# Five blocks per retention head, rotations counted by chunk, HGRN heads of 10 and 11 slots, ten Strassen pairs in the input projection

## The reference

```python
def _layer(...):
    h = _rms_norm(x, g_pre_mix)
    z = h @ w_in
    q_a, k_a, v_a, g_a, q_b, f_b, i_b, g_b, m_a, m_b = _split_cols(z)
    qa = _rope(q_a, pos); ka = _rope(k_a, pos) * (RET_DK ** -0.5)
    o_a, s_ret_new = _retention(qa, ka, va, s_ret, ret_chunk)
    y_a = (silu(g_a) * _head_rms(o_a)) @ w_a
    f = lbh + (1.0 - lbh) * sigmoid(f_b)
    o_b, s_hg_new = _hgrn2(qb, 1.0 - f, vb, jnp.log(f), s_hg, hg_block)
    y_b = (silu(g_b) * _head_rms(o_b)) @ w_b
    mix = sigmoid(m_a) * y_a + sigmoid(m_b) * y_b
    x = x + _rms_norm(mix @ w_out, g_post_mix)
    u = square(relu(_rms_norm(x, g_pre_ffn) @ w_up))
    return x + _rms_norm(u @ w_down, g_post_ffn), s_ret_new, s_hg_new
```

## Time and profile before

| | |
|---|---|
| median of 3 runs | 2351.37 us (2348.11 to 2351.53) |
| the profiled execution | 2349.41 us, its span 2347.6 us |
| mean granted TensorE clock | 0.998 |
| TensorE busy | 2325.4 us, 99% of the span |
| VectorE busy | 1378.4 us, 59% |
| ScalarE busy | 818.0 us, 35% |
| GpSimd busy | 477.9 us, 20% |

### The profile page before, as it was taken

One profiled execution on the slowest core, in us unless ns is written; L12 is line 12 of the kernel. 1 busy time (PEld: TensorE's weight loads), 2 busy tenths in 40 slices (PEclk: granted clock), 3 DMA queues, 4 the chain that ended last, 5 costly groups with the idle time before them and its releaser, 6 DMA issues. The chain is left out here.

```text
span 2347.6 us, 37061 instructions
## 1 busy us (share of the span) xinstructions
PE 2325.4 (99%) x14240; PEld 2184.5 (93%) x14240; DVE 1378.4 (59%) x2562; ACT 818.0 (35%) x1552; POOL 477.9 (20%) x732
## 2 busy tenths in 40 slices
PE   8999999999999999999999999999999999999998
PEld 7899999999999999999999999988999999888886
DVE  7434355362636777777776434556755556777575
ACT  5223232323222333333232332333555554333233
POOL 1000022221206666566655000000000000000002
PEclk9999999999999999999999999999999999999999
DMA  5212455353724343344334634222434436533424
GB/s 196 85 57 103 145 181 173 123 200 115 234 93 158 116 130 113 114 128 133 108 115 143 203 106 140 100 100 82 150 112 152 137 123 250 191 117 125 170 72 143
DMA packets 256044, 319.23 MB, mean 136 GB/s; under 512 B 10005, under 2 KB 200217, under 8 KB 255769
## 3 DMA queue, kind: packets, MB, share of 16 engines
q1 hardware_dynamic: 255464, 315.67, 40.1%
q0 software_dynamic: 432, 1.57, 0.4%
HBM read 205.53 MB, written 111.67 MB: 135 GB/s over the span
## 5 line engine op out<-in xcount | busy, mean ns | idle before, releaser
L942 PE MATMUL bank<-XH,WHI 128*128 128x384 f32 x1776 | 609.9, 343 | 1.6 <-issue 0.9
L944 PE MATMUL bank<-XH,WLO 128*128 128x384 f32 x1776 | 594.7, 335 | 0.0
L943 PE MATMUL bank<-XL,WHI 128*128 128x384 f32 x1776 | 593.9, 334 | 0.0
L942 PEld LDWEIGHTS bank<-XH,WHI 128*128 128x128 f32 x1776 | 333.8, 188 | 5.6 <-issue 2.4
L943 PEld LDWEIGHTS bank<-XL,WHI 128*128 128x128 f32 x1776 | 333.9, 188 | 0.8
L944 PEld LDWEIGHTS bank<-XH,WLO 128*128 128x128 f32 x1776 | 333.3, 188 | 0.0
L1396 ACT ACTIVATE ZST<-bank 128x384 f32<-128x384 f32 x180 | 88.3, 492 | 377.6 <-PE bank L944 371.8
L1330 PE MATMUL bank<-WSH,USH 128*128 128x512 f32 x448 | 175.3, 391 | 1.0 <-issue 1.0
L1332 PE MATMUL bank<-WSH,USL 128*128 128x512 f32 x448 | 175.3, 391 | 0.0
L1331 PE MATMUL bank<-WSL,USH 128*128 128x512 f32 x448 | 175.1, 391 | 0.0
L1396 ACT ACTIVATE WHI<-WRAW 128x1024 fp32r<-128x1024 f32 (+1 forms) x161 | 135.2, 842 | 114.0 <-PE bank L1057 70.3
(11 more groups left out here) (282 smaller groups left out, 5007.1 us busy)
## 6 DMA issues: line engine op xcount, KB each, us to landing
WRAW<-in_w_in SPq DMA_DIRECT2D x80, 512.0 KB, 4.6
scratch_z<-ZST SPq DMA_DIRECT2D x60, 576.0 KB, 3.2
UOP<-scratch_uq SPq DMA_DIRECT2D x28, 1024.0 KB, 7.4
WRAW<-in_w_up SPq DMA_DIRECT2D x32, 512.0 KB, 5.5
scratch_uq<-U SPq DMA_DIRECT2D x16, 1024.0 KB, 4.0
WQ<-in_w_down SPq DMA_DIRECT2D x16, 1024.0 KB, 5.2
scratch_uq<-SU SPq DMA_DIRECT2D x16, 768.0 KB, 5.5
HZ<-scratch_z SPq DMA_DIRECT2D x63, 192.0 KB, 2.9
```

What stands on the lines that cost most here:

```text
L942: pe.matmul(psum[c][:, 0:CH], WHI[p][:, k, :], XH[:, k, s], start=(k == 0), stop=False)
L943: pe.matmul(psum[c][:, 0:CH], WHI[p][:, k, :], XL[:, k, s], start=False, stop=False)
L944: last = pe.matmul(psum[c][:, 0:CH], WLO[p][:, k, :], XH[:, k, s], start=False, stop=(k == KT - 1))
```

## The change

NZ goes from 6 to 10: eight blocks that were plain become four Strassen pairs. Retention heads have five blocks (15 slots, RET_A = 4), and the two blocks of the gap stay as HG_START = 6 slots. HGRN heads have 10 and 11 slots in turn with pieces in slots 0 to 8; with 10 slots the last `out_t` of a head stands in slot 0 of the next. All loops over heads are unrolled. The rotation of q's chunk 0 moves to the end of the head before, chunks of q and k alternate over slots 0 to 4, and q_ok and k_ok count chunks. S8A gets memory of its own, KZ8 takes that of RTMP; ZK and ZV are loaded earlier. GpSimd's chunk 0 of the rotation of k moves to the end of the head before.

```diff
-RET_BLOCKS = 6
-RET_SLOTS = RET_BLOCKS * NC
-HG_BLOCKS = 4
-HG_SLOTS = HG_BLOCKS * NC
-RA = 7
-HG_A = (0, 1, 2, 4, 5, 6, 7, 8, 9)
-R_GATE = (7, 8, 13)
-H_GATE = (0, 2, 6)
+RET_LEN = (5, 5, 5, 5)
+RET_AT = (0, 5, 10, 15)
+RET_BLOCKS = sum(RET_LEN)
+HG_BLOCKS = 30
+HG_START = 6
+HG_LEN = (10, 11, 10, 11, 10, 11, 10, 11)
+HG_AT = [None] * HG_START + [(h, s) for h, n in enumerate(HG_LEN) for s in range(n)]
+RET_A = tuple(NC * n - 11 for n in RET_LEN)
+R_GATE = (1, 2, 6)
+H_GATE = (1, 2, 6)
...
-GAP = 2
-NZ = 7 - GAP // 2
+NZ = (72 - 2 - RET_BLOCKS - HG_BLOCKS) // 2
...
-        S8A = ZK[:, :, :].rearrange("p a t -> p (a t)")[:, 0:4 * 2 * RD].rearrange("p (b d e) -> p b d e", b=4, d=2)
-        KZ8 = [sb(f"KZ8{i}", [P, RD], F32, pr) for i in range(2)]
+        S8A = sb("S8A", [P, 4, 2, RD], F32, pr)
+        KZ8 = [RTMP[:, :, :].rearrange("p a n -> p (a n)")[:, b * RD:(b + 1) * RD] for b in range(2)]
...
+        def hg_slots():
+
+            for q, at in enumerate(HG_AT):
+                yield NHB + q // NC, q % NC, *(at or (None, None))
+
+        def hg_out(h, s):
+
+            if h is None:
+                return None
+            if s == 0:
+                return (h - 1, NT - 1) if h and HG_LEN[h - 1] == NT + 1 else None
+            return (h, s - 2) if 2 <= s < NT + 2 else None
...
+                    if j == late + 3 and h < RH - 1:
+                        sp.wait_ge(R.k_ok, 3 * h + 3)
+                        sp.wait_ge(R.q_ok, 3 * h + 3)
+                        z_stored(6 * h + 9 - 2 * NZ)
+                        load_rk(h + 1)
...
+                if t % TPC == 0:
+                    pe.wait_ge(R.q_ok, 3 * h + t // TPC + 1)
+                    pe.wait_ge(R.k_ok, 3 * h + t // TPC + 1)
                 if t == 0:
-                    pe.wait_ge(R.in_[2], 16 * h + 16)
-                    pe.wait_ge(R.q_ok, h + 1)
-                    pe.wait_ge(R.k_ok, h + 1)
                     pe.wait_ge(R.kz8, 2 * h + 1)
                     pe.wait_ge(R.st_ev, 16 * h + 1)
                 pe.wait_ge(R.kv, 8 * h + t + 1)
...
-            with dve.Fori(0, RH) as h:
-                for s in range(RET_SLOTS):
+            for h in range(RH):
+                RA = RET_A[h]
+                for s in range(NC * RET_LEN[h]):
                     j, c = divmod(s, NC)
-                    n = 2 + RET_BLOCKS * h + j
+                    n = 2 + RET_AT[h] + j
                     if c == 0:
-                        wlo_block(n + 1, (j + 1) % 2)
-                    if s < 3:
+                        wlo_block(n + 1, (n + 1) % 2)
+                    if s == 0 and h == 0:
+                        dve.wait_ge(R.in_[0], 32)
+                        rotate_q(0, 0)
+                    if s in (0, 2, 4):
                         if s == 0:
-                            dve.wait_ge(R.in_[0], 32 * h + 32)
-                        rotate_q(h, s)
-                    if s == 3:
-                        dve.wait_ge(R.in_[1], 16 * h + 16)
-                        for c in range(NC):
-                            rotate_k0(c)
+                            dve.wait_ge(R.in_[1], 16 * h + 16)
+                        rotate_k0(s // 2)
                         dve.sem_inc(R.q_ok, 1)
+                    if s in (1, 3):
+                        rotate_q(h, s // 2 + 1)
                     for t in range(NT):
                         if s == RA + t:
                             if t == 0:
@@ -2161,6 +2181,9 @@
                             dve.wait_ge(R.sc, 9 * h + t + 1)
                             dve.wait_ge(R.st_full, 16 * h + (t if t >= 2 else 1))
                             dve.tensor_tensor(ATT[t % 2][:, :], PSC[:, 0:P], DM[:, t // NTP, :], ALU.mult).then_inc(R.att, 1)
+                    if s == NC * RET_LEN[h] - 1 and h < RH - 1:
+                        dve.wait_ge(R.in_[0], 32 * h + 64)
+                        rotate_q(h + 1, 0)
...
+            for n, c, h, s in hg_slots():
+                end = HG_LEN[-1] - s if h == HH - 1 else None
+                if c == 0 and s != NT:
+                    wlo_block(n + 1, (n + 1) % 2)
+                if n == NHB and c == 0:
                     dve.wait_ge(c_in2, 48)
                     forget(0, 0)
                     prep_q(0, 0, 0)
                     prep_q(0, 0, 1)
                     dve.wait_ge(R.s8_st[0], 32 * RH + 16)
                     prep_q(0, 0, 2)
-                if n == NHB - GAP + 1:
+                if n == NHB + 1 and c == 0:
                     ret_done(dve)
                     forget(0, 1)
                     prep_q(1, 1, 0)
-            wlo_block(NHB + 1, 1)
+                if h is None:
+                    continue
+                if s == 0:
+                    ch.reset()
+                if s < NT:
+                    weights(h, s)
+                if end == 1:
+                    for x in range(6, 11):
+                        piece(x)
+                if hg_out(h, s):
+                    gated(H, *hg_out(h, s), 1)
+                if 1 <= s < NT:
+                    hg_state(h, s - 1)
+                if 1 <= s < NT + 1:
+                    head_ms(H, h, s - 1, HD)
+                if s == NT:
+                    hg_state(h, NT - 1)
+                    if c == 0:
+                        wlo_block(n + 1, (n + 1) % 2)
+                if s < 2:
+                    prep_q(1, (h + 1) % 2, s + 1)
+                if s == 2:
+                    forget(h, 2)
+                if 3 <= s <= 5:
+                    prep_q(2, h % 2, s - 3)
+                if h < HH - 1:
+                    if s == 6:
+                        forget(h + 1, 0)
+                    if 6 <= s <= 8:
+                        prep_q(0, (h + 1) % 2, s - 6)
+                    if s == 9:
+                        forget(h + 1, 1)
+                        prep_q(1, h % 2, 0)
...
+            def rotate_k1(c):
+
+                s = slice(c * CH, (c + 1) * CH)
+                cs, sn = CS[:, 0, s], CS[:, 1, s]
+                pool.tensor_tensor(PTMP[:, 0, :], ZK[:, 0, s], sn, ALU.mult)
+                ch(pool.tensor_tensor(PTMP[:, 1, :], ZK[:, 1, s], cs, ALU.mult))
+                ch(pool.tensor_tensor(KR[:, 1, s], PTMP[:, 0, :], PTMP[:, 1, :], ALU.add))
+                pool.sem_inc(R.k_ok, 1)
+
+            pool.wait_ge(R.in_[1], 16)
+            for c in range(NC):
+                rotate_k1(c)
+            for h in range(RH):
+                gate(R, h, 0, 2, ZG[0][:, :, :])
                 for t in range(NT):
+                    if t == NT - 1 and h < RH - 1:
+                        pool.wait_ge(R.in_[1], 16 * h + 32)
+                        pool.wait_ge(R.att, 9 * h + 10)
+                        rotate_k1(0)
                     head_rs(R, h, t)
+                    if t == 0:
+                        gate(R, h, 1, 2, ZG[1][:, :, :])
                     if t == 4:
                         gate(R, h, 2, 2, ZG[0][:, :, :])
+                if h < RH - 1:
+                    for c in range(1, NC):
+                        rotate_k1(c)
...
+            for h in range(HH):
+                prep_k(h, 1, (h + 1) % 2, {5: lambda: hgate(h, 0)})
+                head_rs(H, h, 0)
+                hgate(h, 1)
+                head_rs(H, h, 1)
+                head_rs(H, h, 2)
+                pool.wait_ge(H.att, 9 * h + 4)
+                prep_k(h, 2, h % 2, {4: rs(h, 3)})
+                head_rs(H, h, 4)
+                hgate(h, 2)
+                if h < HH - 1:
+                    pool.wait_ge(H.att, 9 * h + 7)
+                    prep_k(h + 1, 0, (h + 1) % 2, {0: rs(h, 5), 3: rs(h, 6), 6: rs(h, 7)})
+                    pool.wait_ge(H.att, 9 * h + 10)
```

More of the change, by code:

```diff
@@ L658, in _ @@
             for h in range(RH):
-                for j in range(RET_BLOCKS):
-                    n = 2 + RET_BLOCKS * h + j
+                late = RET_LEN[h] - 5
+                for j in range(RET_LEN[h]):
+                    n = 2 + RET_AT[h] + j
                     load_w(n + 2)
@@ L690, in _ @@
                         sp.dma_start(ZG[0][:, :, :], ret_z(h, 3)[:, :, 0:CH]).then_inc(R.g_in[0], 16)
[L691 to L693 removed]
+                    if j == late + 1:
+                        sp.dma_start(ZG[1][:, :, :], ret_z(h, 3)[:, :, CH:2 * CH]).then_inc(R.g_in[1], 16)
+                        if h:
+                            sp.wait_ge(R.s8_st[0], 32 * h + 16)
                         for d in range(2):
@@ L724, in _ @@
                 ret_store(h, 2)
-            for n in range(NHB - GAP, NHB):
-                load_w(n + 2)
-                store_z(n - 1)
             def load_ua(c):
@@ new lines, in _ @@
+                if s in (3, 6, 9):
+                    sp.wait_ge(H.att, 9 * h + s + 1)
+                    if h < HH - 1:
+                        if s == 3:
+                            z_stored(30 + 4 * h - 2 * NZ)
+                        load_q(h + 1, s // 3 - 1)
+                    else:
+                        load_ua(s // 3 - 1)
+                if s in (5, 8):
```

(68 more changed lines are left out.)

313 lines of the change are left out of this document (96 added, 217 removed).

## The result

The changed kernel takes 2359.1 us (median of 6 runs, 2357.3 to 2360.0), the kernel before 2350.5 (6 runs, 2348.1 to 2351.5). The ratio is 1.0036, interval 1.0026 to 1.0046: **slower by 0.36%**, about 8.6 us. The profiled execution took 2357.8 us, with a span of 2355.7 (before: 2349.4 and 2347.6).

What follows compares the result with a forecast made beforehand. TensorE's own queue was taken to bound the kernel; -11.9 - 0.9 + 5.6 + 1.7 + 7.6 + 1.4 = +3.5 on the profiled 2349.4 gave 2352.9, or 2354.9 us as median; range 2339 to 2364.

Steps and rivals of the forecast that it cites:

- Pairs for slots, -11.9: TensorE's own queue: 24 plain slots leave retention and HGRN heads, four Strassen pairs of 22.25 come in: -11.9 us.
- First head, wait of +5.6: First retention head: TensorE waits before ret_a 1's scores for ATT 0, behind VectorE's whole rotation: +5.6 us.
- Clock, +1.7: First retention head: TensorE's clock may fall to half after the long wait: +1.7 us, between 0 and 3.4.
- WLO stall gone, -0.9: First retention head: TensorE's present wait for WLO before 308.51 disappears: -0.9 us.
- Retention heads 1 to 3 covered by 2.1: Retention heads 1 to 3: ATT 0 written at T + 23.9, wanted at T + 26.0, so no wait.
- the slower rival: Retention heads 1 to 3: VectorE's rotation reaches ATT 0 too late, three waits of 3 us each: 2364; chance 0.22.
- HGRN, +7.6 at out_t 0 by scale 0: HGRN heads 1, 3, 5, 7: late prep_k(h, 1) delays ScalarE's scale 0, so TensorE waits at out_t 0: +7.6 us.
- out_t 7, +1.4: All HGRN heads but the last: scale 7 comes 0.2 us after TensorE reaches out_t 7: +1.4 us in all.
- scale 5: HGRN heads but the last: ScalarE's scale 5 reckoned just in time, with 0 us to spare.
- my own sign: Whole kernel: the prediction is wrong if, among other things, a wait shows up that is not on its list.

Runs made afterwards that it cites:

- The retention part alone: Changed kernel with five-block retention heads and rotation by chunk, but twelve slots in every HGRN head and eight Strassen pairs: 2354.3 us, ratio 1.0012.
- with ATT 0 ahead: Changed kernel, first retention head: rotate_k0 1 moved behind ATT 0 on VectorE, rotate_q 2 and rotate_k0 2 three slots later: 2347.7 us, ratio 0.9987.
- with six blocks per head: Changed kernel with six-block retention heads (rotation by chunk kept), HGRN heads of ten and eleven slots, eight Strassen pairs: 2352.0 us, ratio 1.0003.

## Why the prediction was right or wrong, point by point

The time came out at 2359.1 for the 2354.9 forecast: inside the range, and of the three outcomes slower, to which I had given 0.34; the likeliest by my chances, the same, had 0.40 and did not come. Worked out on the profiled execution it is 2357.8 for 2352.9, 4.9 too low.

- **Pairs for slots, -11.9: right.** Four pairs came in at 88.71 instead of 89.0, and an undisturbed retention head takes 93.3 to 93.45, 12.3 under the 105.70 of before instead of 12.48.
- **First head, wait of +5.6: right in mechanism, place and releaser, too small by 4.1.** TensorE asked when I said, 26.14 after the first plain slot for 26.0. ATT 0 was ready 35.8 after it for 31.6. Three terms were off. ZQ landed 6.28 after the first plain slot and I had carried over 4.48 from the old trace: 1.8. ZK came 1.22 after rotate_q 0 had ended, for 0.46: 0.8. And GpSimd's gate now meets rotate_k0 1, 2.08 for 0.55: 1.5. The sum had counted contention as a fixed 11.4 us of GpSimd work, and had left out that the gate, too, comes two slots earlier (24.2 us after the first plain slot, 33.2 before). The retention part alone shows the first two apart from the third: where ZQ lands at 4.8 and ZK 0.4 after rotate_q 0 the wait is 7.5, which is 5.6, 0.4 for ZQ and the gate, which there meets rotate_q 2 at 354.30, 2.17 for 0.55.
- **Clock, +1.7: right, at 2.0.** The fall I had put between none and two stretches is there, and the size follows from how much of it carries work: 4.07 us.
- **WLO stall gone, -0.9: right.** In the changed kernel it would lie inside the wait for ATT 0, and with ATT 0 ahead it is not there either; with six blocks per head 0.2 of it is there again.
- **Retention heads 1 to 3 covered by 2.1: right.** ATT 0 of head 1 is written at 501.1 where TensorE would have asked at 503.6, 2.4 to spare. So the slower rival, cover failing there, did not happen, although the result was slower.
- **HGRN, +7.6 at out_t 0 by scale 0: the sum nearly right, the cause wrong.** prep_k(h, 1) did start at the head's start + 4.4, as reckoned. It then took 11.8 and not 12.8, and scale 0 was ready at +18.4 for +19.6. In its place came the wait for ATT 0, which I had put at 0.05: VectorE had it at +11.4, not +10.0 (asked at +10.3). The term at fault is the length of VectorE's prep_q beside GpSimd's prep_k: the copy and five multiplies ahead of ATT 0 take 4.7 us from 850.44 on, and 3.6 in the kernel before (from 1017.56 on), where they met other instructions of GpSimd. The copy takes 1.07 for 0.35, and the multiplies at 851.54, 852.31 and 853.82 take 0.73, 1.05 and 0.65 where the same shapes take 0.35 undisturbed. Together: four waits with what goes with them give 6.0 (7.24 for 5.75 from piece 0 to piece 1), eleven stalls 3.5, and the last head's wait of 1.2 is gone; with the -51.0 for slots that is -42.7, measured -42.3, where I had -42.0. The sum came out by luck: two errors against each other.
- **out_t 7, +1.4: wrong.** None. The stalls sit at out_t 5 (seven) and out_t 3 (four). For scale 5 I had written 0 to spare, and it was short by 0.3.
- **By my own sign, wrong here:** a wait that was not on the list (before piece 1) did show up, and so did the stalls at out_t 3 and out_t 5; the waits listed at out_t 0 and out_t 7 did not.
- **What was on no list either:** the opening, +0.95, and 0.96 less behind the heads. The first is not the change's: in the profiled executions of all the kernels here the first pair starts between 147.3 and 150.2. The second seems to be: behind the heads come 1042.3 us in eleven of the twelve kernels that carry the change or a part of it (the twelfth, the retention part, has one slot of 4.2 more there), and 1043.3 in the kernel before, where TensorE waits 0.8 for HR of VectorE (L1935) at 1527.4. Why that wait is gone was not tried.

So the step that failed is the size of the first head's wait, and in it the assumption that loads and GpSimd's other work keep the distances of the old trace. Had it come at 5.6, the time would have been 2355.

## What to carry to other kernels

When a change takes cover away, list for each engine not how much it has to do before the new due time but in what order it does it: here all of 16 us came back by letting the one instruction that TensorE waits for pass work that is due slots later. Where two engines slow each other, work that moves relative to the other's changes length; count which instructions will meet, and don't carry durations or landing times over from the old order. And a wait moved behind an event inherits that event's delay: check what the next consumer needs first.
